# A two-block transformer with routed experts on one core: single-block sums for 64-slot experts, a router fed part by part, both token halves chosen in one step, slot lists behind the first weights

## The reference

```python
def swiglu_2(x, w1, w3, w2):
    return (jax.nn.silu(x @ w1) * (x @ w3)) @ w2

def moe_ffn(u, w_router, b_router, w1, w3, w2, ws1, ws3, ws2):
    scores = jax.nn.sigmoid((xf @ w_router).astype(jnp.float32))
    biased = scores + b_router.astype(jnp.float32)
    grouped = biased.reshape(T, N_GROUPS, N_EXPERTS // N_GROUPS)       # 8 groups of 8
    group_score = jnp.sum(lax.top_k(grouped, 2)[0], axis=-1)
    _, top_groups = lax.top_k(group_score, TOPK_GROUPS)                # 4 groups
    ...
    _, idx = lax.top_k(jnp.where(expert_mask, biased, NEG_INF_2), TOP_K)
    w = jnp.take_along_axis(scores, idx, axis=-1)
    w = w / (jnp.sum(w, axis=-1, keepdims=True) + 1e-20) * ROUTED_SCALE
    ...
    y = lax.map(expert_block, ...)      # each token's 8 experts, times w
    routed = jax.ops.segment_sum(y.reshape(n_slots, D), slot_tok, num_segments=T + 1)[:T]
    shared = swiglu_2(xf, ws1, ws3, ws2)
    return (routed + shared).reshape(B, S, D)
```

## Time and profile before

| | |
|---|---|
| median of 3 runs | 3883.58 us (3872.92 to 3886.76) |
| the profiled execution | 3885.12 us |
| its span, first to last instruction | 3883.1 us |
| TensorE matmuls / weight loads busy | 93% / 80% |
| VectorE, ScalarE, GpSimdE busy | 60%, 38%, 6% |
| data moved | 842.2 MB, 217 GB/s in the mean |
| mean granted TensorE clock | 0.957 |
| chain that ended last | TensorE 75%, DMA 13%, VectorE 7% |

### The profile page before, as it was taken

The page is one execution under the profiler, slowest core; times in us unless marked ns, Lnnn a source line. Parts: engine busy times, 40 slices in busy tenths (PEclk is TensorE's granted clock), DMA queues, the critical chain, the costliest instruction groups (busy, mean ns, idle before and its releaser), DMA issues.

```text
span 3883.1 us, 54052 instructions
## 1 busy us (share of the span) xinstructions
PE 3620.0 (93%) x21765; PEld 3090.0 (80%) x21765; DVE 2346.8 (60%) x3545; ACT 1483.6 (38%) x2208; POOL 244.4 (6%) x335
## 2 busy tenths in 40 slices
PE   5998899998899998889999999999988999999999
PEld 2997799996699786779986666678777999666666
DVE  6774375775377475356566666656644656666665
ACT  1432243432143213133345555531322334555554
POOL 3010010010001001000000000000000000000000
PEclk9998899998899998979999999999988999999999
DMA  7785176684178635235569999975522556999995
GB/s 244 255 295 177 57 268 211 233 298 163 28 253 297 201 119 189 73 137 180 191 224 302 309 310 311 307 231 176 168 71 100 191 193 197 313 302 310 300 308 182
DMA packets 580171, 842.21 MB, mean 217 GB/s; under 512 B 22685, under 2 KB 489732, under 8 KB 578676
## 3 DMA queue, kind: packets, MB, share of 16 engines
q1 hardware_dynamic: 514508, 665.85, 51.8%
q0 software_dynamic: 40896, 146.83, 11.2%
q10 hardware_dynamic: 24552, 26.57, 2.6%
HBM read 835.85 MB, written 3.33 MB: 216 GB/s over the span
## 4 chain that ended last, share of the span: by engine, by line
PE 75%; DMA 13%; DVE 7%; ACT 2%; issue 2%; SPq 1%; DVEq 0%; POOL 0%; ACTq 0%
PE bank L971 13%; PE bank L876 12%; PE bank L877 11%; PE bank L878 11%; DMA ring<-in_w 9%; PE bank L1314 7%; DMA wmod<-in_w_mod 3%; PE bank L1183 2%; PE bank L1326 2%; PE bank L1279 2%; PE bank L1281 2%; PE bank L1280 2%; PE bank L871 1%; DVE ring_lo L2546 1%; PE bank L1297 1%
## 5 line engine op out<-in xcount | busy, mean ns | idle before, releaser
L878 PE MATMUL bank<-hh,ring_lo 128*128 128x256 f32 (+1 forms) x2176 | 623.7, 287 | 0.0
L876 PE MATMUL bank<-hh,hi 128*128 128x256 f32 (+1 forms) x1984 | 566.9, 286 | 16.8 <-issue 12.3
L877 PE MATMUL bank<-h_lo,hi 128*128 128x256 f32 (+1 forms) x1984 | 565.8, 285 | 0.0
L971 PE MATMUL bank<-h,ring 128*128 128x256 f32 x2432 | 554.9, 388 | 8.4 <-ACT h L1493 8.4
L971 PEld LDWEIGHTS bank<-h,ring 128*128 128x128 f32 x2432 | 475.6, 196 | 80.0 <-issue 11.8
L878 PEld LDWEIGHTS bank<-hh,ring_lo 128*128 128x128 f32 (+1 forms) x2176 | 422.1, 194 | 0.0
L876 PEld LDWEIGHTS bank<-hh,hi 128*128 128x128 f32 (+1 forms) x1984 | 381.5, 192 | 19.9 <-issue 15.3
L877 PEld LDWEIGHTS bank<-h_lo,hi 128*128 128x128 f32 (+1 forms) x1984 | 381.4, 192 | 0.0
L876 PE MATMUL bank<-hid,hi 128*128 128x256 f32 (+1 forms) x1248 | 355.9, 285 | 0.0
L877 PE MATMUL bank<-hid_lo,hi 128*128 128x256 f32 (+1 forms) x1248 | 354.9, 284 | 0.0
L878 PE MATMUL bank<-hid,ring_lo 128*128 128x256 f32 (+1 forms) x1088 | 309.5, 284 | 0.0
(11 more groups left out here) (370 smaller groups left out, 6928.5 us busy)
## 6 DMA issues: line engine op xcount, KB each, us to landing
ring<-in_w SPq DMA_DIRECT2D x258, 1024.0 KB, 12.8
ring<-in_ffn_w SPq DMA_DIRECT2D x120, 1024.0 KB, 10.6
wmod<-in_w_mod POOLq DMA_DIRECT2D x216, 512.0 KB, 5.5
far_up<-in_w SPq DMA_DIRECT2D x84, 1024.0 KB, 11.4
ring<-in_w_in SPq DMA_DIRECT2D x74, 1024.0 KB, 7.3
work<-in_w SPq DMA_DIRECT2D x42, 1024.0 KB, 5.5
ring<-in_w_out SPq DMA_DIRECT2D x16, 1024.0 KB, 5.1
ring<-in_w_mod SPq DMA_DIRECT2D x12, 1024.0 KB, 12.8
```

The costliest lines, as they stand in the source:

```text
L876: pe.matmul(o, w_hi, x_hi, start=start, stop=False, skip_group_check=True)
L877: pe.matmul(o, w_hi, x_lo, start=False, stop=False, skip_group_check=True)
L878: return pe.matmul(o, w_lo, x_hi, start=False, stop=stop, skip_group_check=True)
L971: ins = pe.matmul(o[:, half * T:(half + 1) * T], l_, r_, start=(k == 0), stop=(k == KD - 1))
```

## The change

It does five things in each routed layer.

1. `router` on TensorE takes each part of h as it comes: two logit matmuls and two transposes a part. ScalarE makes hh as copies of h after all eight parts.
2. VectorE's choice treats both token halves with one instruction a step, but for max, replace and the last scale.
3. The slot lists move: TensorE's `count_places` and `turn_places` go to either side of the second half of the first dense expert's up matmuls, and the batches are spread over the dense units 2 to 5 by a table, LISTED. ScalarE's store of the places and the first loads of them move into units 2 and 3.
4. WIDE_FROM goes from 16 to 15 and NARROW_FROM from 32 to 31. So there are 15 dense experts, 16 wide and 33 narrow ones; 49 lists in 13 batches.
5. For a narrow unit VectorE writes the low half of og into rows 64 to 127 beside the high half, and spread repeats its 64 rows there (own_few), so that `scatter` needs one matmul of 128 rows in place of two of 64.

```diff
-WIDE_FROM, NARROW_FROM = 16, 32
+WIDE_FROM, NARROW_FROM = 15, 31
+BATCHES = [range(i, min(i + 4, GATHERED)) for i in range(0, GATHERED, 4)]
+LISTED = {(2 + i // 2, i % 2): range(2 * i, min(2 * i + 2, len(BATCHES))) for i in range((len(BATCHES) + 1) // 2)}
...
             def router(sec, X):
+                pe.wait_ge(router_in, 16 * (l + 1))
                 for k in range(KD):
                     pe.wait_ge(h_ready, 8 * s + k + 1)
-                pe.wait_ge(router_in, 16 * (l + 1))
-                for b in range(TB):
-                    for k in range(KD):
-                        ins = pe.matmul(... h[:, k, b * P:(b + 1) * P], wr[:, k, :], ...)
-                ins.then_inc(X["logits"], 1)
-                for b in range(TB):
-                    for k in range(KD):
+                    for b in range(TB):
+                        ins = pe.matmul(... h[:, k, b * P:(b + 1) * P], wr[:, k, :], ...)
+                    if k == KD - 1:
+                        ins.then_inc(X["logits"], 1)
+                    for b in range(TB):
                         ins = pe.transpose(...)
...
                 def scatter(n):
-                        for part in range(2):
-                            ins = pe.matmul(o, og[0:m, part, d * P:(d + 1) * P], spread[0:m, p % 2, :], ...)
+                        for part in range(parts):
+                            ins = pe.matmul(o, og[:, part, d * P:(d + 1) * P], spread[:, p % 2, :], ...)
...
                 down_dense(0, 0)
+                finish(0)
+                up_dense(1, 0)
                 count_places(X)
-                finish(0)
+                up_dense(1, 1)
                 turn_places(X)
-                sum_slots(X, range(0, GATHERED // 8))
-                up_dense(1, 0)
-                sum_slots(X, range(GATHERED // 8, GATHERED // 4))
-                up_dense(1, 1)
                 down_dense(1, 0)
...
                         finish(n - 1)
+                        sum_slots(X, LISTED.get((n, 0), ()))
                         up_dense(n, 1)
+                        sum_slots(X, LISTED.get((n, 1), ()))
...
@@ ScalarE: norm, router, routed @@
-                    if split:
-                        act.activation(hh[:, k, :], h[:, k, :], ACT.Identity, bias=shift)
                     act.activation(h[:, k, :], h[:, k, :], ACT.Identity, bias=shift).then_inc(h_ready, 1)
+                for k in range(KD):
+                    act.wait_ge(h_ready, KD * sec["s"] + k + 1)
+                    act.activation(hh[:, k, :], h[:, k, :], ACT.Copy).then_inc(X["hh"], 1)
+                        if n == 2:
+                            act.wait_ge(*X("copied", 1))
+                            act.dma_start(places_dram.ap()[l], ...)
...
@@ VectorE: out_lo, routed @@
+                        low = og[:, 1, c] if m == WIDE else og[m:P, 0, c]
+                        if n == 1:
+                            place_tokens(X)
+                        pick_slots(X, LISTED.get((n, 1), ()))
```

More of the change, by code:

```diff
@@ L70, with nth @@
 GATHERED = N_EXPERTS - WIDE_FROM
+BATCHES = [range(i, min(i + 4, GATHERED)) for i in range(0, GATHERED, 4)]
+LISTED = {(2 + i // 2, i % 2): range(2 * i, min(2 * i + 2, len(BATCHES))) for i in range((len(BATCHES) + 1) // 2)}
 def routed_order():
     gathered = []
-    for i in range(WIDE_FROM):
+    for i in range(NARROW_FROM - WIDE_FROM):
         gathered += [("wide", WIDE_FROM + i), ("narrow", NARROW_FROM + 2 * i), ("narrow", NARROW_FROM + 2 * i + 1)]
-    order = [("shared", -1)] + [("dense", i) for i in range(WIDE_FROM - 1)] + gathered
-    order.append(("dense", WIDE_FROM - 1))
-    return order
+    gathered.append(("narrow", N_EXPERTS - 1))
+    return [("shared", -1)] + [("dense", i) for i in range(WIDE_FROM - 1)] + gathered + [("dense", WIDE_FROM - 1)]
 ORDER = routed_order()
+def nth(layer, i, total):
+    return 16 * (layer * ((total + 1 - i % 2) // 2) + i // 2 + 1)
 def gathers(n):
@@ L585, in build @@
                     oms=2, ostd=2, suba=4, zs=8, sp=8, pre=24, suf=8, arg=8, aexp=8, fin=8, gsig=1, merged=1)
-        ROUTE = dict(logits=1, sig=1, rows=1, taken=4, chosen=1, gt=1, sorted=1, ranked=1, masked=1, counted=1, placed=1,
-                     turned=1, copied=1, picks=2 * GATHERED // 4, summed=GATHERED // 4, slots=1)
+        ROUTE = dict(hh=KD, logits=1, sig=1, rows=1, taken=4, chosen=1, gt=1, sorted=1, ranked=1, masked=1, counted=1, placed=1,
+                     turned=1, copied=1, picks=2 * len(BATCHES), summed=len(BATCHES), slots=1)
         class Signals:
@@ L1242, in sum_slots @@
                     pe.wait_ge(*X("picks", 2 * i + 2))
-                    for r in range(4):
-                        e = 4 * i + r
+                    for r, e in enumerate(BATCHES[i]):
                         for b in range(TB):
@@ L1319, in scatter @@
                 def scatter(n):
-                    p, m = GATHER_NO[n], slots(n)
+                    p, parts = GATHER_NO[n], 2 if slots(n) == WIDE else 1
                     pe.wait_ge(og_done, 2 * (g0 + p + 1))
@@ L1324, in scatter @@
                         o = bank[4 + d // 2][:, (d % 2) * T:(d % 2 + 1) * T]
-                        for part in range(2):
-                            ins = pe.matmul(o, og[0:m, part, d * P:(d + 1) * P], spread[0:m, p % 2, :], start=False, stop=False, skip_group_check=True)
+                        for part in range(parts):
+                            ins = pe.matmul(o, og[:, part, d * P:(d + 1) * P], spread[:, p % 2, :], start=False, stop=False, skip_group_check=True)
                     ins.then_inc(scattered, 1)
@@ new lines, in router @@
+                masked, left = rt[:, 10:12, :], rt[:, 6:8, :]
+                m3, b3 = (a.rearrange("p b (g e) -> p (b g) e", e=G) for a in (masked, biased))
+                then(dve.tensor_tensor(gt, others, mine, ALU.is_gt))
+                then(dve.tensor_tensor(eq, others, mine, ALU.is_equal))
+                then(dve.tensor_tensor(eq, eq, ties, ALU.mult))
+                then(dve.tensor_tensor(gt, gt, eq, ALU.add))
+                then(dve.tensor_reduce(above, rt[:, 6:8, :].rearrange("p b (g j) -> p (b g) j", j=G), AX, ALU.add))
@@ new lines, in router @@
+                then(dve.tensor_scalar(keep, above, 4.0, None, ALU.is_lt))
+                then(dve.tensor_scalar(off, keep, -NEG, NEG, ALU.mult, ALU.add))
+                then(dve.tensor_tensor(m3, b3, keep.unsqueeze(2).to_broadcast([P, TB * G, G]), ALU.mult))
+                then(dve.tensor_tensor(m3, m3, off.unsqueeze(2).to_broadcast([P, TB * G, G]), ALU.add))
+                for b in range(TB):
+                    ins = dve.max(top8[:, b * G:(b + 1) * G], masked[:, b, :])
+                then(ins)
@@ new lines, in router @@
+                for b in range(TB):
+                    ins = dve.match_replace(left[:, b, :], top8[:, b * G:(b + 1) * G], masked[:, b, :], -3e38)
+                then(ins)
+                then(dve.tensor_tensor(left, left, masked, ALU.not_equal))
+                then(dve.tensor_tensor(left, left, sc, ALU.mult))
+                then(dve.tensor_reduce(total, left, AX, ALU.add))
+                then(dve.tensor_scalar(total, total, 1e-20, None, ALU.add))
+                then(dve.reciprocal(total, total))
@@ L2460, in router @@
+                for b in range(TB):
+                    ins = dve.tensor_scalar(rt[:, 8 + b, :], left[:, b, :], total[:, b:b + 1], 2.5, ALU.mult, ALU.mult)
+                then(ins)
                 dve.tensor_scalar(rt[:, 4:6, :], rt[:, 8:10, :], 0.0, None, ALU.not_equal).then_inc(X["chosen"], 1)
@@ L2580, in spread_slots @@
                     p = GATHER_NO[n]
[L2581 removed]
+                    dve.wait_ge(places_in[p % 2], nth(l, p, GATHERED))
                     if g0 + p >= 2:
                         dve.wait_ge(scattered, g0 + p - 1)
[L2584 removed]
+                    dve.tensor_scalar(spread[:, p % 2, :], places[p % 2], own if slots(n) == WIDE else own_few, None, ALU.is_equal).then_inc(spread_done, 1)
                 rank_experts(X)
```

80 lines of the change are left out of this document (32 added, 48 removed).

## The result

| | before | after |
|---|---|---|
| median (9 runs each) | 3880.81 us | 3847.22 us (3842.09 to 3865.89) |
| ratio, with 95% interval | 1 | 0.9922 [0.9909, 0.9935] |
| span of the profiled execution | 3883.1 us | 3843.9 us |

The change makes the kernel 0.8% faster, by 33.6 us. The forecast was 3808 us; the result lies at the upper edge of the range and 7 us from rival R1 (3840). As the experiments show, it lies there for a reason other than R1's.

A forecast was written before the change was run, and what follows sets the result against it. It saw short waiting steps at the start, TensorE busy throughout the dense experts, TensorE and DMA both nearly full in the gathered ones. Per layer -5.4 -20.6 +11.3 +1.2 -7.0 -18 = -38.5; 3885.1 - 77 = 3808 us; range 3775 to 3848.

The forecast's parts named there:

- R1: Rival, gathered experts: the DMA bounds them, so the one-block scatter gives only 2.1 us a layer; 3840 us; chance 0.23.
- part 5: Narrow gathered experts' scatter in one block: 1.0 us saved per group of three, -18 us a layer (-2 to -29).
- First issue to mark: First expert's first weight issue to the first dense expert's first down matmul: 44.1 us falls to 23.5, -20.6 a layer.
- Parts 1 and 2 alone: Router by parts and both token halves chosen at once: -5.4 us a layer (-3 to -7).
- R5: Rival, layer start: shared expert fills what the router gives; router and choice give 0, lists -18; 3824 us; chance 0.05.
- The lists: Slot lists inside the dense experts: 98 thin matmuls, 16 in 1.84 us, +11.3 us a layer, +1.2 for the clock.
- R3: Rival, dense experts: the clock falls with each group of thin matmuls, 27 us a layer; 3860 us; chance 0.08.
- R4: Rival: clock stays low through the four dense experts carrying lists, 52 us plus 9 for thin matmuls; 3928 us; chance 0.03.
- Dense to narrow: Rank 15 gathered instead of dense: -17.28 us against one more narrow unit of 10.3, -7.0 a layer (-5.5 to -7.5).
- I take 0.4 for a group: Gathered experts: part of the scatter's saving given back per group because TensorE waits for turned rows, 0.4 us.
- the share of 0.97 says 3%: Gathered experts: the DMA share leaves transfers 3% of room, 1.1 us a group; the GB/s suggested up to 15%.
- R2: Rival, gathered experts: TensorE bounds them, the one-block scatter gives 29 us a layer; 3786 us; chance 0.13.

The follow-up runs named there:

- before_ups_first: The kernel before, with only SyncE's load order changed: the next gathered expert's up slabs ahead of this one's down slab; 3848.8 us, ratio 0.9919.
- ups_first: The changed kernel, with the next gathered expert's up slabs issued ahead of this expert's down slab; 3745.3 us, ratio 0.9647.
- rows_first: The changed kernel, old load order, but ScalarE and VectorE turn this expert's rows before splitting the next expert's first up slab; 3827.9 us, ratio 0.9847.
- two_blocks: The changed kernel with the scatter of two blocks put back, all else the same; 3841.2 us, ratio 0.9900.

## Why the prediction was right and wrong

By the prediction's own steps, in us per layer. "After" compares the profiled executions of before and after, layer 0 / layer 1; "loop open" compares before_ups_first and ups_first. Single starts are read from TensorE's timeline, from the norm's first matmul on.

| step | forecast | after | loop open |
|---|---|---|---|
| norm to first wide expert (parts 1, 2, 3, and the dense expert of part 4) | -30.8 | -32.1 / -33.8 | -32.3 / -33.8 |
| 15 of the 16 groups of gathered experts (part 5) | -15.0 | **+11.2 / +3.8** | -21.8 / -20.3 |
| last wide expert to the end of the last down matmul (the 16th group, one more narrow expert, two short scatters) | +7.2 | +6.9 / +7.4 | +6.2 / +6.2 |
| sum | -38.6 | -14.0 / -22.6 | -47.9 / -47.9 |

**The start: right.** Router's first matmul right behind the first part of h: yes. Choice and first issue 5 us earlier: the choice reaches TensorE at 1693.47 instead of 1705.11, of which 5.6 us are the run's earlier start, so 6.0; forecast 6.7. First issue to mark: 25.2 us in layer 0 and 23.0 in layer 1, against 23.5; before 44.1. The norm to the mark: 25.7 us less, forecast 26.0. Parts 1 and 2 alone: 5.4 forecast, 4.8 and 7.4 by the profiles, so R5, which gave them nothing, is out.

**The lists: right.** 16 thin matmuls in 1.84 us, no fall of the clock in the dense stretch. R3 and R4 are out. The stretch from the mark on fell by 6.4 us, where the sum had -4.8.

**Dense to narrow: right in kind.** 7.0 forecast, 8.4 and 5.4 by the profiles with the loop open, 6.9 in the mean; 9.2 by the medians.

**Part 5: wrong, and this is the whole miss.** The step that failed is "Between 0 and 1.68 us a group; I take 1.0, near the share's figure". With the loop open a group is 1.46 us shorter, below the sum's upper bound of 1.68 but near it, though TensorE's matmuls save 1.51 us a group and not 2.08. Two terms failed. The first is what is given back: "I take 0.4 for a group", read from one unit. The waits for turned rows grew from 14.0 to 35.8 us in 14 groups, 1.56 us a group, and the lower clock, to which the sum gave nothing here, came on top. The second is the room of the transfers, "the share of 0.97 says 3%". The earlier trace rows already had a share of 1.08 at 364 GB/s, so 0.97 was no distance to a limit; the 15% that the prediction read from the GB/s, and set aside, was the better reading. And the lower bound was "no gain", where the result was a loss. A shorter unit ran into late weights more often; such a wait passed through ScalarE's queue to TensorE, often lowered its clock, and postponed the issue of the next three slabs. That this path is the cause is shown by the runs that open it: reordered loads take the waits, the falls of the clock and the loss away (57.9 us gained for 11.7 lost), and rows_first takes the waits for rows and the falls of the clock away by ScalarE's and VectorE's order alone. In the 15 groups of layer 0, two_blocks against after: 13 us less of busy TensorE, of which 22.6 were to be had (508.9 - 486.3 with the loop open), so that some 9.5 went to the lower clock (an estimate from these sums; the rows have 0.97 against 0.99); and 21.4 us more of idle.

**R1: right in its time (3840), wrong in its reason.** It said that the transfers bound the gathered experts, and priced part 5 at nothing. But the DMA was not at its limit: a change of order gave 334 GB/s. R1's own figure of 35.4 us for a group was not a floor either: 32.6. And it could not tell that the scatter costs 10 us. So the nearness of 3847 to its 3840 is luck. R2, which had TensorE set the pace, is the picture of the kernel with reordered loads (1.46 us a group where it had 1.68), not of this one.

The prediction cited the Trainium skill ("Trainium Kernel Development and Optimization", Performance Expectations) on weight-load busy time as the good measure of TensorE. The section means the distance to roofline, and names it beside MFU (the arithmetic done, as a share of the peak); the prediction read it as slack. In ups_first it reads 327.1 of 488.9 us, 67%, as in before; yet there, with one block against two, a group got 1.46 us shorter for 1.5 us less of busy matmul time (509 - 486 us in 15 groups), and TensorE's waits were the same three in both, 3.9 and 3.8 us. So these rows don't bear it out as a measure of slack.

The Trainium skill ("Perfetto Trace Analysis", Identifying the Most-Contended Engine) says to judge DMA not by occupancy, which sixteen engines make misleading, but by its use of HBM. The runs agree: 299 GB/s at a share of 0.96 became 334 at 1.03. The Trainium skill ("DMA: Bandwidth & Descriptors", Specifications) gives about 358 GB/s for a core, as half of what two cores share. By it the 309 GB/s of the earlier trace rows would be 86%, an estimate. This kernel runs on one core, and the earlier trace rows measured 364 GB/s, more than that figure; by the measured rate the 309 are 85%.

## What to carry to other kernels

Where two engines both look full, ask what a step's end *triggers*: here the finish issues the next weights, and anything that makes it uneven comes back as late weights. Before taking work from the busy engine, see that each queue asks first for what is needed first, and as soon as its slot is free; here that one reordering was worth 107 us and turned a 10 us loss of the same scatter into a gain of 58. And let the lower bound of a gain lie below zero where a shorter step can bring its neighbour into waits: here these waits lowered TensorE's clock too.

## What was not expected of the hardware

- The share of DMA time is no measure of what is left: 0.95 to 0.97 at 298 to 306 GB/s, 1.00 at 321, 1.01 at 318, 1.03 at 334, for the same weights and the same kinds of transfer, and 1.08 at 364 in the earlier trace rows.
- After a wait of 3.56 us TensorE did eight matmuls at a mean granted clock of 0.55: 6.44 us instead of 3.62. Of 23 waits over 1.5 us, 13 were followed by such a fall, some already at 2.0 us (5.32 us for 3.62), and one of 3.64 us was not. What decides this was not looked for.

Open: whether some 2 us on the first of two up slabs is all of the 67 us that the place in the queue brings. No run separates it from the 1.1 us that the two are also issued earlier, being first in the batch. A run of ScalarE's order together with the order of loads was not made; with TensorE busy 99.5% of the stretch it has little to find there.
